# Latent attention: the value products of a head's last two tiles, with their gates, behind the next head's scores

## The chip, the cores and the metric

The kernel runs on one core of a Trainium2 chip. Times are device microseconds (us) from launch to end. TensorE (PE) does matrix products and transposes into PSUM, an accumulation memory of eight banks here; VectorE (DVE), ScalarE (ACT) and GpSimd (POOL) work on what stands in PSUM (GpSimd only on SBUF) and in SBUF. Each engine takes its own instructions in the order in which the program lists them and waits at semaphores for the others.

## The reference, cut to what matters

Two layers: first multi-head latent attention (MLA), then sparse attention. The change is in the first. For 512 tokens and 16 heads it computes, after low-rank projections and norms:

```python
def causal_block_attention(q, k, v, scale):
    for start in range(0, S, Q_BLOCK):          # four tiles of 128 queries
        s = jnp.einsum('bqhd,bkhd->bhqk', q[:, start:end], k[:, :end]) * scale
        p = jax.nn.softmax(jnp.where(mask, s, -jnp.inf), axis=-1)
        outs.append(jnp.einsum('bhqk,bkhd->bqhd', p.astype(v.dtype), v[:, :end]))
...
    o = causal_block_attention(q, k, v, MLA_QK ** -0.5)
    o = o.reshape(B, S, MLA_HEADS * MLA_V) * jax.nn.silu(z)
    return o @ w_out
```

## The kernel before

The program is a list of instructions per engine, written by hand; nothing is reordered by a scheduler. Products that need more than one pass of precision are done by `mm3` (lines 93 to 95): high by high, high by low and low by high part. So each weight and each activation is split into a high part (ScalarE, a copy) and a low part (VectorE or GpSimd, raw minus high).

The 16 heads run as a pipeline over steps h = 0 to 15. Each step works on three heads at once and on four tiles i = 0 to 3 of 128 tokens:

- `scores(h, a, i)` (L684 to L690): products of queries by keys into one of two banks. scores(h, 0) waits for the low parts of head h's four tiles (`x_free`).
- `turn(h + 1, i)` (L674): transposes of the next head's normed queries and keys.
- `values(h, i)` (L707): i + 1 products of transposed probabilities by values into a single bank, `o_bank`. It waits for the transposed probabilities (`pt_ready`) and for the gate of the tile before it (`o_free`), which reads that bank.
- `turn_probs(h, i)` (L699): i + 1 transposes of the probabilities, after their exponential.
- `project(h + 2, a, i)`: 15 products that make queries, keys and values of the head after the next; tile t waits for `p_free` of tile t - 2.

`split_weights(h + 3)` makes that head's weights in high (ScalarE L985) and low parts (VectorE L1356), in the steps 0 to 12. Heads after 15 don't exist: from step 14 nothing is projected, in step 15 nothing is turned.

On VectorE, a step does for each tile: `maximum` (L1379) of the scores, `low(h + 1)` (L1373), in tile 0 the split of the weights, in tile 1 `probs_out(h, 0)` (L1384, probabilities to SBUF), from tile 2 on `gate(h, i - 2)` (L1389 reciprocal of the row sum, L1392 product with the silu path) and `scale(h + 2, i - 1)` (L1364, L1366: norm factor and gain on queries and keys). At a step's end follow probs_out(h, 3), gate(h, 2), scale(h + 2, 3), gate(h, 3). The factor of a scale comes from GpSimd (L1221, L1222), which needs the squares that ScalarE sums over the projection (L993, L995). GpSimd also rotates the scaled queries (L1234 to L1239), two tiles at a time. On ScalarE, a tile of a step is `exponential` (L1009), `high(h + 1)` (L1002), in tile 0 the split, then probs_out of tiles 1 and 2 (L1015) and `stats(h + 2)`.

Of `step` on TensorE the end is:

```python
                        turn_probs(h, 3)
                        if h == H - 1:
                            turn_o(0)
                        values(h, 2)
                        if h == H - 1:
                            turn_o(1)
                        values(h, 3)
```

`turn_o` (L738) transposes the gated output for the output projection.

Of the kernel before, what the change touches and what calls it, by code (L numbers as in the profile page):

```python
# [32 lines left out]
H = 16  # L33
# [64 lines left out]
def trunk(nc, x, positions, inv_freq, norm_g, mla_w_in, mla_g_cq, mla_w_uq, mla_g_ckv, mla_w_ukv,  # L98
          mla_g_q, mla_g_k, mla_w_out, nsa_w_in, nsa_g_q, nsa_g_k, nsa_pe_k, nsa_w1_k, nsa_w2_k,
          nsa_pe_v, nsa_w1_v, nsa_w2_v, nsa_w_out, out):  # L100
    with ExitStack() as whole:
# [281 lines left out]
        with ExitStack() as layer:  # L383
            z_sb = at_slab("z_sb", 0, [P, NT, ZZ])
            with ExitStack() as ctx:
# [197 lines left out]
                def _(pe):  # L583
# [64 lines left out]
                    def project(n, a, t):  # L648

                        if t == 0:  # L650
                            pe.wait_ge(wh_ready, n + 1)
                        if n == 0 and t == 0:
                            pe.wait_ge(c_lo_made, KQ + KKV)
                        if 4 * n + t > 1:
                            pe.wait_ge(p_free, 4 * n + t - 1)
                        tok = slice(t * P, (t + 1) * P)
                        for k in range(KQ):
                            mm3(nc, p_bank[t % 2][:, 0:WQ], (c_hi[:, k, tok], c_lo[:, k, tok]),
                                (wq_of(wh_hi[a], k), wq_of(wh_lo[a], k)), start=k == 0, stop=k == KQ - 1)
                        for k in range(KKV):  # L660
                            last = mm3(nc, p_bank[t % 2][:, WQ:WQ + WKV],
                                       (c_hi[:, KQ + k, tok], c_lo[:, KQ + k, tok]),
                                       (wkv_of(wh_hi[a], k), wkv_of(wh_lo[a], k)), start=k == 0, stop=k == KKV - 1)
                        last.then_inc(p_done, 1)

                    def turn(n, t):

                        if t % 2 == 0:
                            pe.wait_ge(qk_rotated, 2 * n + t // 2 + 1)
                        if 4 * n + t > 1:  # L670
                            pe.wait_ge(x_free, 4 * n + t - 1)
                        for part in range(4):
                            src = (qn, kn)[part // 2][:, t, (part % 2) * HQK:(part % 2 + 1) * HQK]
                            last = nc.tensor.transpose(x_bank[t % 2][0:HQK, part * P:(part + 1) * P], src, ident[:, :])  # L674
                        last.then_inc(x_done, 1)

                    def scores(h, a, i):
                        if i == 0:
                            pe.wait_ge(x_free, 4 * h + 4)
                        if h == 0 and i == 0:  # L680
                            pe.wait_ge(z_left, NT * (NCH - 2))
                        tok, keys = slice(i * P, (i + 1) * P), (i + 1) * P

                        dst = score_bank[i % 2]  # L684
                        for part in range(2):
                            mm3(nc, dst[:, 0:keys], (qkT_hi[a][:, part, tok], qkT_lo[a][:, part, tok]),
                                (qkT_hi[a][:, 2 + part, 0:keys], qkT_lo[a][:, 2 + part, 0:keys]),
                                start=part == 0, stop=False)
                        nc.tensor.matmul(dst[:, tok], identb[:, :], causal[:, :], start=False,
                                         stop=True).then_inc(s_done, 1)  # L690

                    def turn_probs(h, i):


                        pe.wait_ge(exp_done, 4 * h + i + 1)
                        if i == NT - 1:
                            pe.wait_ge(pt_ready, 4 * h + i)
                        for j in range(i + 1):
                            last = nc.tensor.transpose(pt_bank[:, j * P:(j + 1) * P],  # L699
                                                       prob[:, i % 2, j * P:(j + 1) * P], ident[:, :])  # L700
                        last.then_inc(t_done, 1)

                    def values(h, i):
                        pe.wait_ge(pt_ready, 4 * h + i + 1)
                        pe.wait_ge(o_free, 4 * h + i + 1)
                        for j in range(i + 1):
                            last = nc.tensor.matmul(o_bank[:, 0:DV0], probT[:, i % 2, j * P:(j + 1) * P],  # L707
                                                    v_all[:, j, h * DV0:(h + 1) * DV0], start=j == 0, stop=j == i)
                        last.then_inc(pv_done, 1)

                    def step(h, a, x, p):
                        for i in range(NT):
                            scores(h, a, i)
                            if x:
                                turn(h + 1, i)
                            if i >= 2:
                                values(h, i - 2)
                            if i >= 1:
                                turn_probs(h, i - 1)
                            if p:  # L720
                                project(h + 2, a, i)
                        turn_probs(h, 3)
                        if h == H - 1:
                            turn_o(0)
                        values(h, 2)
                        if h == H - 1:
                            turn_o(1)
                        values(h, 3)

                    def turn_o(k):  # L730

                        if k == 0:
                            pe.wait_ge(p_free, 4 * H)
                        if k >= 4:
                            pe.wait_ge(o_lo_made, k - 3)
                        pe.wait_ge(o_free, 4 * k + 5)
                        for t in range(NT):
                            last = nc.tensor.transpose(bank[4 + k % 4][:, t * P:(t + 1) * P],  # L738
                                                       z_sb[:, t, k * P:(k + 1) * P], ident[:, :])
                        last.then_inc(o_turned, 1)  # L740
# [544 lines left out]
                def _(dve):  # L1285
# [68 lines left out]
                    def split_weights(n, a):  # L1354
                        dve.wait_ge(wh_hi_made, n + 1)
                        nc.vector.tensor_tensor(wh_lo[a][:, :], wh_raw[:, :], wh_hi[a][:, :].bitcast(F32),  # L1356
                                                ALU.subtract).then_inc(wh_ready, 1)
# [12 lines left out]
                    def low(n, a, t):  # L1370
                        dve.wait_ge(x_hi, 4 * n + t + 1)
                        at = slice(t * P, (t + 1) * P)
                        nc.vector.tensor_tensor(qkT_lo[a][:, :, at],  # L1373
                                                x_bank[t % 2][0:HQK, :].rearrange("p (a t) -> p a t", a=4),
                                                qkT_hi[a][:, :, at].bitcast(F32), ALU.subtract).then_inc(x_free, 1)

                    def maximum(h, a, i):
                        dve.wait_ge(s_done, 4 * h + i + 1)
                        nc.vector.tensor_reduce(negmax[:, a, i:i + 1], score_bank[i % 2][:, 0:(i + 1) * P], AX.X,  # L1379
                                                ALU.max, negate=True).then_inc(max_done, 1)  # L1380
# [6 lines left out]
                    def gate(h, a, i):  # L1387

                        o.link(nc.vector.reciprocal(rinv[:, i:i + 1], rowsum[:, a, i:i + 1]))  # L1389
                        dve.wait_ge(pv_done, 4 * h + i + 1)  # L1390
                        at = z_sb[:, i, h * DV0:(h + 1) * DV0]
                        nc.vector.scalar_tensor_tensor(at, o_bank[:, 0:DV0], rinv[:, i:i + 1], at, ALU.mult,  # L1392
                                                       ALU.mult).then_inc(o_free, 1)

                    def step(h, a, x, p):
                        for i in range(NT):
                            maximum(h, a, i)
                            if x:
                                low(h + 1, 1 - a, i)
                            if i == 0 and h + 3 < H:  # L1400
                                split_weights(h + 3, 1 - a)
                            if i == 1:
                                probs_out(h, 0)
                            if i >= 2:
                                gate(h, a, i - 2)
                            if p and i >= 1:
                                scale(h + 2, i - 1)
                        probs_out(h, 3)
                        gate(h, a, 2)
                        if p:  # L1410
                            scale(h + 2, 3)
                        gate(h, a, 3)


                    nc.vector.memset(rinv[:, :], 1.0).then_inc(o_free, 1)
# [494 lines left out]
```

## Time and profile before

| | us |
|---|---|
| median of 3 runs | 1056.43 |
| the three runs | 1054.86, 1056.43, 1056.91 |
| the profiled execution | 1056.62 |
| its span, first to last instruction | 1054.8 |
| TensorE busy in the span | 1009.9 |
| VectorE, ScalarE, GpSimd busy | 454.8, 398.8, 407.5 |

The span is 1.8 us shorter than the time of its own execution. The kernel's first 165 us are loads, the input projection and the projection of the first two heads. The heads' steps follow until about 431 us, then the output projection, the second layer's input projection, its attention and its output projection. A "start" below is in us from the span's start. Matmuls are pipelined: one of 128 rows by 128 columns is listed with about 0.27 us, but the next one starts 0.11 us after it, and the profile counts the longer figure as busy. An fp32 product of that size is recorded as two instructions, so that the eight of values(h, 3) stand for four products.

### The profile page before, as it was taken

The numbers are of one execution on the slowest core, as the hardware profiler recorded it, in microseconds if no ns is written. First come the engines' busy times: TensorE is split into PE (matmuls) and PEld (weight loads), VectorE is DVE, ScalarE is ACT, GpSimd is POOL, SyncE is SP. The second block draws the span as 40 slices with busy tenths as digits, with TensorE's granted clock in tenths as the row PEclk, the third lists the DMA queues.
The fourth block names the chain that finished last, engine by engine and source line by source line (L and its number), as shares of the span: only waits on it lengthen the run. The fifth ranks groups of instructions, "written<-read, shape, count | busy, mean of one in ns | idle before, by whom it ended". The sixth has DMA issues, their size and how long they took to land. (4 is left out here: it accounts for less than half of the span.)

```text
span 1054.8 us, 16083 instructions
## 1 busy us (share of the span) xinstructions
PE 1009.9 (96%) x6262; PEld 867.6 (82%) x6262; DVE 454.8 (43%) x1217; ACT 398.8 (38%) x948; POOL 407.5 (39%) x548
## 2 busy tenths in 40 slices
PE   4999998999999998999999999999989999999898
PEld 4988888989898987788888877788868888888776
DVE  3331025666656655321111114667645555555511
ACT  4263245555555544431342122344323333333210
POOL 1444436454555543234344234657621111111131
PEclk8999999999999999999999999999989999999899
DMA  5332131101010110222372212222200000000031
GB/s 178 108 120 80 53 93 42 44 22 44 23 43 23 44 41 2 80 80 80 106 153 77 79 40 75 86 85 80 81 1 1 1 1 1 2 1 2 1 109 52
DMA packets 42454, 58.89 MB, mean 56 GB/s; under 512 B 8821, under 2 KB 25482, under 8 KB 42378
## 3 DMA queue, kind: packets, MB, share of 16 engines
q1 hardware_dynamic: 40672, 57.42, 17.5%
q8 instruction: 50, 0.82, 0.3%
q10 hardware_dynamic: 1706, 0.43, 0.2%
q14 instruction: 26, 0.21, 0.1%
HBM read 55.62 MB, written 2.10 MB: 55 GB/s over the span
## 5 line engine op out<-in xcount | busy, mean ns | idle before, releaser
L93 PE MATMUL bank<-w_hi,h_hi 128*128 128x512 f32 (+2 forms) x480 | 188.4, 393 | 6.7 <-DVE h_lo L1295 6.7
L1253 POOL TENSOR_TENSOR w_lo<-w_raw,w_hi 128x2048 fp32r<-128x2048 f32 (+1 forms) x26 | 118.6, 4560 | 173.9 <-ACT w_hi L1039 173.9
L94 PE MATMUL bank<-w_lo,h_hi 128*128 128x512 f32 (+2 forms) x480 | 184.4, 384 | 0.0
L95 PE MATMUL bank<-w_hi,h_lo 128*128 128x512 f32 (+2 forms) x480 | 184.3, 384 | 0.0
L93 PEld LDWEIGHTS bank<-w_hi,h_hi 128*128 128x128 f32 x480 | 91.3, 190 | 26.0 <-DVE w_lo L1290 6.9
L95 PEld LDWEIGHTS bank<-w_hi,h_lo 128*128 128x128 f32 x480 | 91.2, 190 | 17.1
L94 PEld LDWEIGHTS bank<-w_lo,h_hi 128*128 128x128 f32 x480 | 91.4, 191 | 15.5
L93 PE MATMUL bank<-w_hi,c_hi 128*128 128x192 f32 (+1 forms) x320 | 93.8, 293 | 3.3 <-DVE kn L1366 3.3
L95 PE MATMUL bank<-w_hi,c_lo 128*128 128x192 f32 (+1 forms) x320 | 88.8, 278 | 0.0
L94 PE MATMUL bank<-w_lo,c_hi 128*128 128x192 f32 (+1 forms) x320 | 88.5, 276 | 0.0
L1774 POOL TENSOR_TENSOR o_c<-o_c,o_sw 128x256 f32<-128x256 f32 x16 | 11.8, 735 | 186.1 <-DVE o_c L1840 186.1
L1695 PE MATMUL bank<-kvr,probT 128*128 128x65 f32 x640 | 82.1, 276 | 0.0
L1039 ACT ACTIVATE w_hi<-w_raw 128x2048 fp32r<-128x2048 f32 (+1 forms) x26 | 49.2, 1891 | 85.7 <-PE bank L95 85.7
L93 PE MATMUL bank<-w_hi,o_hi 128*128 128x512 f32 x192 | 78.1, 407 | 2.3 <-PEq L1869 1.9
L1695 PEld LDWEIGHTS bank<-kvr,probT 128*128 128x128 f32 x640 | 76.9, 193 | 0.0
L95 PE MATMUL bank<-w_hi,o_lo 128*128 128x512 f32 x192 | 76.5, 398 | 0.0
L94 PE MATMUL bank<-w_lo,o_hi 128*128 128x512 f32 x192 | 76.3, 397 | 0.0
L1198 POOL TENSOR_TENSOR w_lo<-w_raw,w_hi 128x2048 fp32r<-128x2048 f32 (+1 forms) x11 | 46.6, 4236 | 73.9 <-ACT w_hi L926 73.9
L1373 DVE TENSOR_TENSOR qkT_lo<-bank,qkT_hi 96x512 fp32r<-96x512 f32 x64 | 43.9, 687 | 70.0 <-ACT qkT_hi L1002 70.0
L1009 ACT ACTIVATE prob<-bank,negmax 128x128 f32<-128x128 f32 (+1 forms) x64 | 33.8, 528 | 102.5 <-DVE negmax L1379 102.5
L1794 DVE TENSOR_REDUCE negmax<-bank 128x2 f32<-128x256 f32 (+2 forms) x96 | 54.7, 596 | 26.2 <-PE bank L1606 25.1
L1745 ACT ACTIVATE probT<-bank 128x512 f32<-128x512 f32 (+1 forms) x96 | 48.9, 526 | 44.6 <-PE bank L1637 43.0
(255 smaller groups left out, 2284.0 us busy)
## 6 DMA issues: line engine op xcount, KB each, us to landing
w_raw<-in_nsa_w_in SPq DMA_DIRECT2D x10, 1024.0 KB, 5.0
w_raw<-in_mla_w_in SPq DMA_DIRECT2D x8, 1024.0 KB, 5.0
w_raw<-in_mla_w_out SPq DMA_DIRECT2D x8, 1024.0 KB, 5.0
w_raw<-in_nsa_w_in SPq DMA_DIRECT2D x8, 984.0 KB, 5.0
w_raw<-in_mla_w_uq SPq DMA_DIRECT2D x16, 288.0 KB, 3.0
w_raw<-in_mla_w_ukv SPq DMA_DIRECT2D x16, 256.0 KB, 3.3
w_raw<-in_nsa_w_out SPq DMA_DIRECT2D x4, 1024.0 KB, 5.7
w_raw<-in_mla_w_in SPq DMA_DIRECT2D x4, 704.0 KB, 5.0
```

What stands on the lines that cost most here:

```text
L93: nc.tensor.matmul(out, a[0], b[0], start=start, stop=False)
L94: nc.tensor.matmul(out, a[0], b[1], start=False, stop=False)
L95: return nc.tensor.matmul(out, a[1], b[0], start=False, stop=stop)
L1009: nc.scalar.activation(prob[:, i % 2, 0:keys], score_bank[i % 2][:, 0:keys], ACT.Exp, bias=negmax[:, a, i:i + 1], accum_out=rowsum[:, a, i ...
L1039: nc.scalar.activation(w_hi[g % 2][:, :, 0:width], w_raw[g % 2][:, :, 0:width], ACT.Copy).then_inc(m_hi, 1)
L1198: nc.gpsimd.tensor_tensor(w_lo[g % 2][:, :, 0:width], w_raw[g % 2][:, :, 0:width], w_hi[g % 2][:, :, 0:width].bitcast(F32), ALU.subtract). ...
L1253: nc.gpsimd.tensor_tensor(w_lo[g % 2][:, :, 0:width], w_raw[g % 2][:, :, 0:width], w_hi[g % 2][:, :, 0:width].bitcast(F32), ALU.subtract). ...
L1373: nc.vector.tensor_tensor(qkT_lo[a][:, :, at], x_bank[t % 2][0:HQK, :].rearrange("p (a t) -> p a t", a=4), qkT_hi[a][:, :, at].bitcast(F32 ...
L1695: last = nc.tensor.matmul(o_most[:, i, b, :] if i < 3 else o_last[:, b, :], probT[n % 2][:, at:at + P], kvr[:, j, c0:c0 + DV1], start=j == ...
L1745: nc.scalar.activation(probT[n % 2][:, at:at + wide], score_bank[k % 3][:, 0:wide], ACT.Exp).then_inc(exp_done, 1)
L1774: o.link(nc.gpsimd.tensor_tensor(o_c[:, :, :], o_c[:, :, :], o_sw[:, :, 0, :], ALU.add))
L1794: nc.vector.tensor_reduce(negmax[:, n % 2, i, b0:b0 + nb], first_bank[k % 2][:, 0:nb * keys].rearrange("p (b c) -> p b c", b=nb), AX.X, AL ...
```

## The change

On TensorE the value products of tiles 2 and 3 of a head leave the head's end. They are issued in the next step, those of tile 2 behind scores(h + 1, 0) and turn(h + 2, 0), those of tile 3 behind scores(h + 1, 1) and turn(h + 2, 1). On VectorE their gates move likewise: gate(h, 2) behind the next step's tile 0 with its split of weights, gate(h, 3) behind the next step's maximum 1 and low 1. The last head keeps its old order. Nothing else is touched.

```diff
@@ TensorE, step
                             scores(h, a, i)
                             if x:
                                 turn(h + 1, i)
+                            if i < 2 and h:
+                                values(h - 1, i + 2)
                             if i >= 2:
                                 values(h, i - 2)
...
                         turn_probs(h, 3)
                         if h == H - 1:
                             turn_o(0)
-                        values(h, 2)
-                        if h == H - 1:
+                            values(h, 2)
                             turn_o(1)
-                        values(h, 3)
+                            values(h, 3)
@@ VectorE, step
                             if i == 0 and h + 3 < H:
                                 split_weights(h + 3, 1 - a)
+                            if i < 2 and h:
+                                gate(h - 1, 1 - a, i + 2)
                             if i == 1:
                                 probs_out(h, 0)
...
                         probs_out(h, 3)
-                        gate(h, a, 2)
                         if p:
                             scale(h + 2, 3)
-                        gate(h, a, 3)
+                        if h == H - 1:
+                            gate(h, a, 2)
+                            gate(h, a, 3)
```

On TensorE, from the end of head 0 into step 1 (x7 is the seven products of tiles 2 and 3; w_hi and c_hi belong to a projection, qkT to scores, ident with prob or qn to transposes), the difference reads:

```order
@@ -813,5 +813,4 @@
 L95 MATMUL bank<-w_hi,c_lo 128x256
 L699 MATMUL bank<-ident,prob 128x128 x4
-L707 MATMUL bank<-v_all,probT 128x128 x7
 L93 MATMUL bank<-qkT_hi_83 128x128
 L94 MATMUL bank<-qkT_lo_85,qkT_hi_83 128x128
@@ -823,4 +822,5 @@
 L674 MATMUL bank<-ident,qn 96x128 x2
 L674 MATMUL bank<-ident,kn 96x128 x2
+L707 MATMUL bank<-v_all,probT 128x128 x3
 L93 MATMUL bank<-w_hi,c_hi 128x192
 L94 MATMUL bank<-w_lo,c_hi 128x192
```

Four of the seven products (tile 3) stand one projection and one pair of scores further on.

On VectorE, the end of head 0 and the start of step 1, before the change:

```order
105 L1384 COPY probT<-bank 128x512
106 L1389 RECIPROCAL rinv<-rowsum 128x1
107 L1392 SCALAR_TENSOR_TENSOR z_sb<-bank,rinv,z_sb 128x128
108 L1364 SCALAR_TENSOR_TENSOR qn<-bank,ms_qk,gq 128x192
109 L1366 SCALAR_TENSOR_TENSOR kn<-bank,ms_qk,gk 128x128
110 L1389 RECIPROCAL rinv<-rowsum 128x1
111 L1392 SCALAR_TENSOR_TENSOR z_sb<-bank,rinv,z_sb 128x128
112 L1379 TENSOR_REDUCE negmax<-bank 128x1
113 L1373 TENSOR_TENSOR qkT_lo_85<-bank,qkT_hi_83 96x4x128
114 L1356 TENSOR_TENSOR w_lo<-w_raw,w_hi 128x1088
115 L1379 TENSOR_REDUCE negmax<-bank 128x1
```

and with it (its lines are numbered one higher, L1393 for L1392 and so on):

```order
105 L1385 COPY probT<-bank 128x512
106 L1365 SCALAR_TENSOR_TENSOR qn<-bank,ms_qk,gq 128x192
107 L1367 SCALAR_TENSOR_TENSOR kn<-bank,ms_qk,gk 128x128
108 L1380 TENSOR_REDUCE negmax<-bank 128x1
109 L1374 TENSOR_TENSOR qkT_lo_85<-bank,qkT_hi_83 96x4x128
110 L1357 TENSOR_TENSOR w_lo<-w_raw,w_hi 128x1088
111 L1390 RECIPROCAL rinv<-rowsum 128x1
112 L1393 SCALAR_TENSOR_TENSOR z_sb<-bank,rinv,z_sb 128x128
113 L1380 TENSOR_REDUCE negmax<-bank 128x1
```

Head 0's gate of tile 2, two instructions, now follows the split of the weights, and its gate of tile 3 comes four instructions after that.

## Rows read from the trace of the kernel before

**Rows 1.** The page, busy time, share of the span and instructions of each engine

```profile
PE 1009.9 (96%) x6262; PEld 867.6 (82%) x6262; DVE 454.8 (43%) x1217; ACT 398.8 (38%) x948; POOL 407.5 (39%) x548
```

**Rows 2.** One head: length; PE, PEld, DVE, ACT, POOL busy; clock; DMA share; GB/s

```profile
235.60:252.80 17.20, 16.47 (x137) 15.47 (x136) 10.69 (x27) 9.32 (x36) 8.73 (x24) 1.00 0.11 34
```

**Rows 3.** TensorE's waits from 165 to 431 us: releaser, total, times, longest

```profile
PE bank L707 <- DVE z_sb L1392: 11.5, 18, 0.7
```

**Rows 4.** Timeline of TensorE through a head: start, duration, line, operands, idle before

```profile
231.16 0.60 PE L699 MATMUL bank<-ident,prob 128*128 128x128 f32 x4
231.74 0.91 PE L707 MATMUL bank<-v_all,probT 128*128 128x128 f32 x6
233.38 1.13 PE L707 MATMUL bank<-v_all,probT 128*128 128x128 f32 x8 [0.73 <-DVE z_sb L1392]
234.26 0.30 PE L93 MATMUL bank<-qkT_hi 96*128 96x128 f32 x1
...
235.39 0.34 PE L93 MATMUL bank<-w_hi,c_hi 128*128 128x192 f32 x1
...
237.18 0.28 PE L93 MATMUL bank<-qkT_hi 96*128 96x256 f32 x1
...
238.41 0.27 PE L699 MATMUL bank<-ident,prob 128*128 128x128 f32 x1
...
248.36 0.60 PE L699 MATMUL bank<-ident,prob 128*128 128x128 f32 x4
```

**Rows 5.** Timeline of VectorE and GpSimd around the same head end

```profile
230.45 0.69 DVE L1373 TENSOR_TENSOR qkT_lo<-bank,qkT_hi 96x512 fp32r<-96x512 f32 x1 [1.33 <-ACT qkT_hi L1002]
231.06 0.15 DVE L1389 RECIPROCAL rinv<-rowsum 128x1 f32<-128x1 f32 x1
...
232.39 0.70 POOL L1222 TENSOR_TENSOR ms_qk<-ms_qk,minus_half 128x2 f32<-128x2 f32 x1
232.69 0.15 DVE L1389 RECIPROCAL rinv<-rowsum 128x1 f32<-128x1 f32 x1
232.88 0.35 DVE L1392 SCALAR_TENSOR_TENSOR z_sb<-bank,rinv,z_sb 128x128 f32<-128x128 f32 x1
233.19 0.42 DVE L1364 SCALAR_TENSOR_TENSOR qn<-bank,ms_qk,gq 128x192 f32<-128x192 f32 x1
...
233.79 0.15 DVE L1389 RECIPROCAL rinv<-rowsum 128x1 f32<-128x1 f32 x1
...
235.20 0.32 POOL L1239 TENSOR_TENSOR qn<-rotq 128x64 f32<-128x64 f32 x1
```

**Rows 6.** Timeline of VectorE and ScalarE in the next step's first tile

```profile
235.24 0.29 DVE L1379 TENSOR_REDUCE negmax<-bank 128x1 f32<-128x128 f32 x1 [0.28 <-PE bank L689]
235.56 0.37 ACT L1009 ACTIVATE prob<-bank,negmax 128x128 f32<-128x128 f32 x1 [3.36 <-DVE negmax L1379]
...
236.40 1.10 ACT L985 ACTIVATE w_hi<-w_raw 128x1088 fp32r<-128x1088 f32 x1
236.53 0.69 DVE L1373 TENSOR_TENSOR qkT_lo<-bank,qkT_hi 96x512 fp32r<-96x512 f32 x1 [1.00 <-ACT qkT_hi L1002]
...
237.54 1.30 DVE L1356 TENSOR_TENSOR w_lo<-w_raw,w_hi 128x1088 fp32r<-128x1088 f32 x1 [0.32 <-ACT w_hi L985]
...
238.75 0.42 DVE L1379 TENSOR_REDUCE negmax<-bank 128x1 f32<-128x256 f32 x1
```

**Rows 7.** Timeline of TensorE in the last two steps

```profile
416.79 0.63 PE L699 MATMUL bank<-ident,prob 128*128 128x128 f32 x4 [1.25 <-ACT probT L1015]
...
419.98 0.30 PE L93 MATMUL bank<-qkT_hi 96*128 96x128 f32 x1
```

**Rows 8.** Timeline where GpSimd's rotation and VectorE's split of weights overlap

```profile
155.36 1.38 DVE L1356 TENSOR_TENSOR w_lo<-w_raw,w_hi 128x1088 fp32r<-128x1088 f32 x1
...
155.54 1.37 POOL L1235 TENSOR_TENSOR rotq<-qn,tsin 128x64 f32<-128x64 f32 x1
```

**Rows 9.** Busy time by stretch, early in the second layer's attention (columns as rows 2)

```profile
764.00:781.00 17.00, 14.36 (x60) 9.77 (x58) 4.93 (x8) 5.92 (x9) 5.30 (x2) 0.70 0.00 1
```

## The prediction

> **What bounds the kernel now.** I read the busy table first: TensorE is busy 1009.9 of 1054.8 us, every other engine under 44% [rows 1]. So time is lost or won only where TensorE stands still. The change touches the attention of the first layer, the heads between about 165 and 431 us. There the table by stretches shows one head: 17.20 us, of which TensorE is busy 16.47, VectorE 10.69, ScalarE 9.32, GpSimd 8.73, at a granted clock of 1.00 [rows 2]. The five stretches of 17.20 us that I cut from 184 us on agree to the last digit, so the heads repeat exactly and one of them can be worked through for all. The waits of TensorE in this stage are led by one entry: the value products (L707) wait for the gate (L1392), 11.5 us in 18 times [rows 3]. That wait stands at the end of each head.
>
> The timeline of one head end shows it [rows 4]. I count everything from the start of the last probability transposes, turn_probs(h, 3), at 231.16. Four instructions of this kind take 0.44 us (0.11 each: the eight of values(h, 3) run from 233.38 to 234.26). Then values(h, 2) starts at 231.74, 0.14 late, and is issued in 6 x 0.11 = 0.66. values(h, 3) could start at 232.40 and starts at 233.38, 0.98 late: it needs the bank that gate(h, 2) frees, and that gate ends at 232.88 + 0.35 = 233.23 [rows 5]; 0.15 later TensorE goes on. So a head end loses 0.14 + 0.98 = 1.12 us. The profile names 0.73 of it, since it counts a matmul's modelled tail as busy. The check: the pieces of a head, 0.44 (transposes), 1.13 (scores 0 and turn, 234.26 to 235.39), 3.02 (first projection, scores 1, turn, 235.39 to 238.41), 9.95 (from turn_probs(h, 0) to the next turn_probs(h, 3), 238.41 to 248.36) and 0.66 + 0.88 (values) add up to 16.08, and 17.20 - 16.08 = 1.12.
>
> **Part one: what goes.** No arithmetic is added or removed; 15 pairs of value products and their gates move, with no DMA or other issue. In steps 0 to 13 the head end runs straight from the transposes into scores(h+1, 0). That needs low(h+1, 3), which ends at 230.45 + 0.69 = 231.14 [rows 5]; the scores come at 231.60, so 0.46 us are in hand and I put this wait at nothing (what would use up the 0.46 is a later high on ScalarE; bound: 0.1 us). A gain of 1.12 per head end, if nothing else waits.
>
> **Part two: what is late next.** The moved gate(h, 2) now stands on VectorE behind maximum 0, low 0 and the split of the next weights (L1356); the value products of tile 3, now after scores 1 on TensorE, wait for it, and everything on TensorE is queued behind them. When does that gate end? From turn_probs(h, 3) = 0:
> - scale(h+2, 3) starts at 233.19 - 231.16 = 2.03. It is not held by the gate ahead of it but by GpSimd's power, 232.39 + 0.70 = 233.09 [rows 5], so it does not come earlier when that gate leaves. VectorE is free at 233.79, that is 2.63.
> - maximum 0 then starts at once, since its scores are done by 0.44 + 0.94. Before, it waited for TensorE until 235.24. From there the rows run: exponential +0.32, ScalarE's split of the weights +0.84 (behind exponential and high, back to back), VectorE's split +1.14, the next instruction +1.21 [rows 6]. That is 2.63 + 3.51 = 6.14.
> - the gate: reciprocal to product 0.19 (232.69 to 232.88), product 0.35, to TensorE 0.15 [rows 4, 5], 0.68 together when the rounding of the hundredths is spread: 6.14 + 0.68 = 6.82.
> TensorE is ready for values(h, 3) at 0.44 + 1.13 + 0.66 + 3.02 = 5.25. It waits 1.57 us, in place of the 1.12 removed. The new head is 6.82 + 0.88 + 9.95 = 17.65 us against 17.20: **0.45 us longer**, for the 12 heads from turn_probs(0, 3) to turn_probs(12, 3), since split_weights runs in steps 0 to 12: 12 x 0.45 = +5.4 us. After the gate VectorE is behind by some two us, but catches up: maximum 1, low 1, gate(h, 3), probs_out 0 and scale end before TensorE asks for them at its third scores, so no second wait is added in these heads.
>
> **Part three: the last heads.** Step 13 has no split. The gate is then ready for TensorE at 2.63 + 0.32 + 0.97 (exponential to low, 235.56 to 236.53) + 0.61 (low to reciprocal, 230.45 to 231.06) + 0.68 = 5.21 [rows 5, 6], TensorE comes at 5.25: no wait, 1.12 won. In step 14 nothing is projected. TensorE comes to values(13, 3) at 5.25 - 1.79 (the projection, 235.39 to 237.18) + 0.1 = 3.55 and waits 1.66. For the other waits of these two steps I walked the queues: each engine's entries in program order, each with its duration and each release with its delay as in the rows. In step 14 that gives -1.12 (old head end), +1.65 (this wait) and -1.1, because values(14, 0) comes later and finds its probabilities nearly ready (a wait of 1.3 becomes 0.2): 13.1 in place of 13.63 between the transposes (248.36 + 9 x 17.20 = 403.16, to 416.79). Step 15: scores(15, 0) starts at 419.98, 3.19 after the transposes at 416.79; now 0.44 after. The 1.54 of values(14, 2) and (14, 3) comes back behind the scores, where it fills a wait for the exponential of about 0.3. 3.19 - 0.44 - 1.54 + 0.3 = 1.5; the walk gives 1.4. Steps 14 and 15 together: -1.95 [rows 7]. Behind turn_probs(15, 3) the order is unchanged, and later stages just shift.
>
> **The sum:** +5.4 - 1.1 - 1.95 = +2.35 us. On the profiled execution's own 1056.62 us that is 1059.0; the median of the runs, 1056.43, lies 0.19 lower. I take **1058.8 us**. The same walk with the old order gives 17.18 per head against the 17.20 of the trace, so I trust it to about 0.1 us a head, 12 x 0.1 = 1.2 us either way; with the tail's 0.3, +0.8 to +3.9.
>
> **A rule against this change.** The weights' split reads two operands from SBUF, and it moves closer to GpSimd's rotation. Rows: at 155.36, where the two overlap, the split took 1.38 instead of 1.29 to 1.30, and GpSimd's product 1.37 instead of 0.32 [rows 8]. In the heads the rotation ends at 235.20 + 0.32, 4.36 on my clock [rows 5]; the split now starts at 4.93 instead of 6.38. So 0.57 remains and the sum has nothing for it. The Trainium skill (SBUF — State Buffer, "Who interferes with whom") says that a VectorE instruction with two SBUF inputs and a GpSimd instruction that reads SBUF exclude each other, and the one that came second blocks; the row agrees. By that rule a rotation 0.6 later would hold the split, and with it TensorE, for what is left of one GpSimd product.
>
> **Rivals.**
> A, the gate comes in time (not slower). If the gate were free for TensorE by 5.25 instead of 6.82, all of the 1.12 would stay won: 14 x 1.12 = 15.7 and some 1.5 in the last two heads, 1039 us. For it speaks that VectorE is busy only 10.69 of 17.20 us. Against it: its busy share doesn't matter, the queue's order does, and every link is read from a row. The point from which it decides: per head even at 0.45 less, in total even at 0.20 less (2.35 / 12). Full gain 3%; between them (the chain up to 0.4 shorter, 1052 to 1056) 5%.
> B, the chain is longer than the sum, since it is now all on the path: the collision above, at most a GpSimd product of 0.32 per head, 12 x 0.32 = 3.8, giving 1062.6; or the probabilities of the next head waiting too. 10%.
> C, the clock. In the second layer TensorE had a granted clock of 0.70 from 764 to 781 us [rows 9]; half clock is 1.2 GHz, so it lost up to 0.30 x 17 = 5.1 us there. Where such a stretch begins can move with the shift of 2 us, and the runs before differ by 2.05 us (1054.86 to 1056.91). This is no result of the change but widens it by about 1.5 us.
>
> **How the numbers follow.** The likeliest is the forecast, the wait moved and 0.45 longer, 82%: 1058.8, its own range 1056.5 to 1061. A holds 8%, B 10%. The range that holds 8 in 10: 1055.8 to 1061.8. 0.2% is 2.1 us, about what can be told from no change, and my sum lies right at it. The forecast's 82% therefore splits in two: 42% within 0.2%, 40% above. B adds its 10% to slower. A gives 6% faster (below 1054.3) and 2% within. So faster 0.06, same 0.44, slower 0.50.
>
> **What would show it.** In the profile after: a head of 17.6 us instead of 17.20; L707's wait for the gate still the first entry of TensorE's waits, 13 long ones of about 1.2 us by the profile's count (some 0.4 of the 1.57 hidden by the modelled tail); that wait in front of the eight products only, none before scores 0; VectorE's maximum 0 directly behind scale 3; the split's start 4.9 us after the last transposes; step 13 about 16.1 us. Wrong would make it: heads of 16.1 us throughout (A), a split of VectorE that starts later than 5.1 or takes over 1.3 (B), or a second wait, at probs_out 0 or at a projection.

## The result and the profile after

Over 16 runs each, the changed kernel takes 1061.53 us at the median, the kernel before 1056.16. The medians lie 5.4 us apart. The ratio on record, which is not the plain quotient of the two medians, is 1.0041 with a 95% interval of 1.0027 to 1.0055, so 0.41% slower, 4.3 us; the heads of the two profiles, below, differ by 5.1 us. The profiled execution took 1062.37 us, with a span of 1060.6 us.

The waits of TensorE in the heads come first. In the rows, an engine's instruction waits for another's; then the total, the number of times and the longest:

```profile
PE bank L707 <- DVE z_sb L1393: 20.0, 14, 1.9
PE bank L93 <- DVE qkT_lo L1374: 1.3, 1, 1.3
```

The wait of [rows 3] is still there, for the same gate, and instead of 11.5 us it now takes 20.0. It has fewer and longer parts: 14 times up to 1.9 us in place of 18 times up to 0.7. The second row is one wait, of the first scores of all, at 166.50; the kernel before has it too (1.25 us at 165.43).

One head by stretch (columns as in [rows 2]), then the stretch of step 14 and four single microseconds inside it:

```profile
251.90:269.64 17.74, 16.28 (x136) 15.41 (x135) 10.72 (x28) 9.32 (x35) 8.78 (x24) 1.00 0.10 32
...
409.97:424.37 14.40, 11.14 (x76) 9.88 (x75) 8.03 (x22) 6.08 (x20) 2.94 (x9) 0.88 0.00 1
...
416.00:417.00 1.00, 1.00 (x9) 1.00 (x9) 0.18 (x1) 0.79 (x3) 0.00 (x0) 0.90 0.00 0
417.00:418.00 1.00, 1.00 (x4) 1.00 (x4) 0.96 (x4) 0.00 (x0) 0.00 (x0) 0.50 0.00 0
419.00:420.00 1.00, 1.00 (x7) 0.99 (x6) 0.28 (x1) 0.68 (x3) 0.00 (x0) 0.50 0.00 0
420.00:421.00 1.00, 1.00 (x6) 0.87 (x5) 0.50 (x1) 0.79 (x2) 0.00 (x0) 0.89 0.00 0
```

A head takes 17.74 us, not 17.20, with a clock of 1.00. In step 14 the granted clock falls to 0.50, which is 1.2 GHz, for about 3.4 us.

The timeline of one head of the kernel after, TensorE first, then the other engines (start, duration, engine, line, operands, idle before). It answers to [rows 4 to 6]:

```profile
251.91 0.60 PE L699 MATMUL bank<-ident,prob 128*128 128x128 f32 x4
...
253.48 0.83 PE L707 MATMUL bank<-v_all,probT 128*128 128x128 f32 x6
...
258.73 1.13 PE L707 MATMUL bank<-v_all,probT 128*128 128x128 f32 x8 [1.46 <-DVE z_sb L1393]
...
259.69 0.27 PE L699 MATMUL bank<-ident,prob 128*128 128x128 f32 x1
...
269.65 0.60 PE L699 MATMUL bank<-ident,prob 128*128 128x128 f32 x4
```

```profile
253.15 0.70 POOL L1223 TENSOR_TENSOR ms_qk<-ms_qk,minus_half 128x2 f32<-128x2 f32 x1
...
253.95 0.42 DVE L1365 SCALAR_TENSOR_TENSOR qn<-bank,ms_qk,gq 128x192 f32<-128x192 f32 x1 [0.42 <-POOL ms_qk L1223]
...
254.54 0.28 DVE L1380 TENSOR_REDUCE negmax<-bank 128x1 f32<-128x128 f32 x1
...
254.85 0.37 ACT L1010 ACTIVATE prob<-bank,negmax 128x128 f32<-128x128 f32 x1 [1.89 <-DVE negmax L1380]
...
255.69 1.11 ACT L986 ACTIVATE w_hi<-w_raw 128x1088 fp32r<-128x1088 f32 x1
...
256.83 1.29 DVE L1357 TENSOR_TENSOR w_lo<-w_raw,w_hi 128x1088 fp32r<-128x1088 f32 x1 [0.32 <-ACT w_hi L986]
...
258.04 0.16 DVE L1390 RECIPROCAL rinv<-rowsum 128x1 f32<-128x1 f32 x1
...
258.23 0.35 DVE L1393 SCALAR_TENSOR_TENSOR z_sb<-bank,rinv,z_sb 128x128 f32<-128x128 f32 x1
```

Read the chain upwards from 258.73. The eight products start 0.15 after the gate's end (258.23 + 0.35). The gate stands directly behind the split, the split waits for ScalarE's part, ScalarE's part stands behind exponential and high, the exponential waits for maximum 0, and maximum 0 starts at once behind the scale, which waits for GpSimd. From the transposes at 251.91 to 258.73 it is 6.82 us.

The time from the last transposes of one head to those of the next, through the stage:

| interval between the x4 transposes | before | after |
|---|---|---|
| heads 0 to 12, twelve intervals | 12 x 17.20 = 206.40 | 213.24 |
| of these: head 2 to 3 | 17.20 | 18.10 |
| of these: the nine from head 3 on | 17.20 | 17.74 or 17.75 |
| head 12 to 13 | 17.20 | 16.10 |
| head 13 to 14 | 13.63 | 14.40 |
| head 14 to 15 | 10.49 | 9.04 |
| sum, head 0 to 15 | 247.72 | 252.78 |

That is +5.06 us in the heads, of the 5.8 us between the two spans. The rest is a later arrival at head 0 by 1.07 (180.63 against 179.56), less 0.3 behind the heads. The later arrival is not the change's: a second profile of the changed kernel arrives at 179.45.

Below, step 13, 14 and 15 stand for the intervals of head 12 to 13, 13 to 14 and 14 to 15, and a scale 3 that VectorE lists at the end of a step runs at the start of the next interval: that of step 13 in head 13 to 14.

### The profile page after: what moved, and what is told of

It is laid out like the page before. It is cut to its first block and busy times, and to the rows that moved or that the text cites. A ratio compares the mean times of both kernels' runs of the same rounds, so it can differ in the third digit from the quotient of the medians.

```text
span 1060.6 us, 16083 instructions
## 1 busy us (share of the span) xinstructions
PE 1007.3 (95%) x6262; PEld 867.7 (82%) x6262; DVE 454.8 (43%) x1217; ACT 398.9 (38%) x948; POOL 408.1 (38%) x548
## 5 line engine op out<-in xcount | busy, mean ns | idle before, releaser
L707 PE MATMUL bank<-v_all,probT 128*128 128x128 f32 x320 | 47.7, 280 | 20.0 <-DVE z_sb L1393 20.0
```

## Experiments

### The gate ahead of the split

```diff
                             if x:
                                 low(h + 1, 1 - a, i)
+                            if i == 0 and h:
+                                gate(h - 1, 1 - a, 2)
                             if i == 0 and h + 3 < H:
                                 split_weights(h + 3, 1 - a)
-                            if i < 2 and h:
-                                gate(h - 1, 1 - a, i + 2)
+                            if i == 1 and h:
+                                gate(h - 1, 1 - a, 3)
```

> The changed kernel with one difference on VectorE: gate(h-1, 2) stands ahead of the weights' split of tile 0, not behind it; TensorE's order is that of the changed kernel. Theory (the gate queued behind the split is what TensorE waits for): the gate is there 5.21 us after the last transposes of the head, TensorE comes at 5.25, so no wait at the eight products, heads of 16.1 to 16.2 us in place of 17.74, and 16 us less than the kernel before: about 1040 us. Rival (the hand-over of the single bank from tile 2 to tile 3 costs TensorE its wait wherever the gate stands): heads stay at 17.2 us or more, 1056 us or more. Second rival (the split itself comes late for the next projection now): no wait at the products, but one of 0.3 us or more before a projection, heads of 16.5.

Measured: 1041.09 us at the median, ratio to before 0.9850 (0.9826 to 0.9874). The heads take 16.10 to 16.14 us (head 2 to 3: 16.47). The table by stretch for one head, and the wait for the gate over all heads:

```profile
261.56:277.66 16.10, 16.10 (x136) 15.39 (x135) 10.62 (x28) 9.32 (x35) 8.63 (x24) 1.00 0.13 37
...
PE bank L707 <- DVE z_sb L1393: 2.5, 4, 1.9
```

TensorE is busy all of the head. The gate comes only just in time: it ends at 266.26 + 0.35 = 266.61, and the eight products start at 266.76, 0.15 later, the delay that they have behind a gate elsewhere. TensorE's order is that of the changed kernel, so the handing over of the bank from tile 2 to tile 3 is free; what cost the time was the place of two VectorE instructions behind a third. Both rivals fall. Step 14 took 14.70 us, not the 13.1 that my walk gives, with a wait of 1.9 us and a clock of 0.88, both as in the changed kernel, where the step takes 14.40.

### Both gates behind the maximum

```diff
                             maximum(h, a, i)
+                            if i < 2 and h:
+                                gate(h - 1, 1 - a, i + 2)
                             if x:
                                 low(h + 1, 1 - a, i)
                             if i == 0 and h + 3 < H:
                                 split_weights(h + 3, 1 - a)
-                            if i < 2 and h:
-                                gate(h - 1, 1 - a, i + 2)
```

> As the one before, but both moved gates stand right behind the maximum of tile 0 and of tile 1, ahead of low. Theory: the gate is there about 1.8 us earlier than TensorE needs it, so the heads are the same 16.1 us, and only step 14, where TensorE comes early, gains: 12.2 to 12.6 us between its transposes in place of 13.1. In all 17 us less than before: 1039 us. If the gate in front of low delays the low parts, a wait shows at scores or at the turn of a head, and the heads are longer than in the run with the gate behind low.

Measured: 1035.77 us, ratio 0.9810 (0.9785 to 0.9834). All heads take 16.02 us, step 14 12.52, and TensorE waits for the gate 0.7 us in all:

```profile
243.30:259.32 16.02, 16.02 (x136) 15.38 (x135) 10.72 (x28) 9.32 (x35) 8.78 (x24) 1.00 0.12 36
...
PE bank L707 <- DVE z_sb L1393: 0.7, 3, 0.3
```

This is the fastest version tried, 20 us under the kernel before: same instructions as the changed kernel, with two of VectorE's in another place. It is 3 us faster than expected. Against the run before, 5.3 us at the median, the two profiles show 3.8 us in the heads (233.65 and 229.82 from head 0 to 15): 1.3 from the other heads, 0.1 shorter each, 2.2 from step 14, whose low clock is absent here, and 0.3 from the late start in head 2 (explained under the changed kernel's second profile), which is now covered. Most of the 0.1 is in the eight products: with the gate well ahead they take 0.89 (248.49 to 249.38), where with the gate just in time they take 0.96 (266.76 to 267.72). The rest of the 5.3 I can't place.

### Only tile 3 moves

```diff
+                            if i == 0 and h:
+                                values(h - 1, 3)
...
                         turn_probs(h, 3)
...
                         values(h, 2)
-                        values(h, 3)
```

On VectorE gate(h, 2) stays at the head's end and gate(h, 3) moves behind the next maximum 0; the last head keeps its old order.

> Half of the change: the value products of tile 2 and their gate stay at the head's end, as before; only those of tile 3 move, and only behind the next head's first scores, with their gate behind maximum 0. Theory (the loss at a head's end is the wait of tile 3 for tile 2's gate, which 1.1 us of scores and turn can fill): the 0.14 before the products of tile 2 stay, the 0.98 goes: heads of 16.2 to 16.3 us, 15 us less than before, about 1041.5 us. Rival (a gate at the head's end costs TensorE the wait, whatever stands between): heads of 17.2.

Measured: 1040.77 us, ratio 0.9854 (0.9831 to 0.9877), heads of 16.21 to 16.23 us, for one of them the transposes from start to start:

```profile
261.52 0.60 PE L699 MATMUL bank<-ident,prob 128*128 128x128 f32 x4
...
277.73 0.60 PE L699 MATMUL bank<-ident,prob 128*128 128x128 f32 x4
```

As expected on each point: 0.14 of the old loss stays, 0.98 goes. So 1.1 us of cover is enough for that hand-over, and the gain needs neither the second projection nor the second scores in between.

### A longer split, in both kernels

```diff
+                        if n > 3:
+                            spare = w_lo[a][:, :, :].rearrange("p k c -> p (k c)")[:, 1088:1488]
+                            nc.vector.tensor_tensor(spare, wh_raw[:, 0:400], wh_hi[a][:, 0:400].bitcast(F32),
+                                                    ALU.subtract)
                         nc.vector.tensor_tensor(wh_lo[a][:, :], wh_raw[:, :], wh_hi[a][:, :].bitcast(F32),
                                                 ALU.subtract).then_inc(wh_ready, 1)
```

> The kernel before with a longer split of the weights on VectorE: from head 4 on a second subtraction of 400 columns, whose result nobody reads, stands in front of the real one (some 0.45 us by the 1.30 for 1088 columns), in 12 steps. Theory: in this kernel nothing that TensorE needs soon stands behind the split, and about 0.5 us are in hand, so heads stay at 17.2 and the time at that of before, within 1 us. Rival (VectorE's own work per head is on TensorE's path in both kernels): 12 x 0.45 = 5 us more.

> The changed kernel with the same longer split. Theory: the split now stands between the last transposes and the gate that TensorE waits for, so every bit of it counts: heads of 17.74 + 0.45 = 18.2 us, 5 to 6 us more than the changed kernel, about 1066.5 us. Rival (the gate's wait hangs on something else of the chain): less than 2 us more.

The added instruction, as the first of these two runs shows it, with the real split behind it:

```profile
240.48 0.58 DVE L1358 TENSOR_TENSOR w_lo<-w_raw,w_hi 128x400 fp32r<-128x400 f32 x1 [0.32 <-ACT w_hi L985]
240.97 1.28 DVE L1360 TENSOR_TENSOR w_lo<-w_raw,w_hi 128x1088 fp32r<-128x1088 f32 x1
```

It holds VectorE for 0.49 us. In the kernel before, heads grew from 17.20 to 17.32 to 17.34, and the time to 1057.37 us (ratio 1.0015, 0.9997 to 1.0034): nearly all of it is hidden, though 0.13 per head is not, so the slack was below the half microsecond that I gave it.

The profile of this run took 1062.23 us, 4.9 above the median of its runs. Its heads don't explain that: two stretches at half clock do, from 167.2 to 170.6 and from 423.2 to 430.1, the second in step 15:

```profile
423.22 2.05 PE L707 MATMUL bank<-v_all,probT 128*128 128x128 f32 x8 [0.60 <-DVE z_sb L1396]
...
420.91:434.29 13.38, 11.37 (x58) 9.95 (x59) 5.15 (x17) 4.92 (x12) 4.52 (x1) 0.74 0.24 80
```

The waits just ahead of the second were 1.26, 0.17 and 0.60 us, and the one ahead of the first 1.25. In the profile of the kernel before the same waits stand at the same places, the clock stays at 1.00, and step 15 takes 10.49.

In the changed kernel, heads of undisturbed clock grew from 17.74 to 18.22, that is by 0.48, the whole of it. So far the theory holds. But the time rose to 1078.53 us (ratio 1.0196, 1.0171 to 1.0220), 17 us and not 5 to 6. The timeline and two neighbouring heads by stretch say why:

```profile
265.28 1.13 PE L707 MATMUL bank<-v_all,probT 128*128 128x128 f32 x8 [1.94 <-DVE z_sb L1397]
...
257.98:277.78 19.80, 17.86 (x137) 17.00 (x136) 11.22 (x29) 9.30 (x35) 9.26 (x24) 0.91 0.09 29
277.78:296.00 18.22, 16.28 (x136) 15.40 (x135) 11.21 (x29) 9.30 (x35) 9.25 (x24) 1.00 0.11 32
```

The first of the two heads lost 1.58 us more at a mean clock of 0.91. Of the twelve intervals eight are like it (19.76 to 19.86) and four like the second. With the wait of 1.46 us in the changed kernel not one head was, in two profiles; with 1.94 two of three are, in one. The added half microsecond was so paid about three times over.

### The changed kernel again

> The changed kernel again, for a second profile. Expected: heads of 17.74 us again, all twelve; step 13 16.1, step 15 9.0. In the first profile step 14 took 14.40 us with a granted clock of one half from 415.0 to 418.4. If that stretch belongs to this kernel, it is there again and the median of these runs is 4 to 5.5 us above before; if it comes and goes, the profile or some of the runs lack it, and step 14 is then 13.1 us. Head 2 took 18.10 because VectorE began a scale 0.36 us late; I expect that at another place or not at all.

Measured: 1061.03 us, ratio 1.0047 (1.0030 to 1.0064). The profile repeats the first within a few hundredths: heads of 17.74 and 17.75, head 2 to 3 again 18.10, step 13 16.11, step 14 14.39 with its low clock, step 15 9.04. (In the first profile that stretch is from 416.8 to 420.2, by its rows above, and not from 415.0 to 418.4 as the expectation has it.) My expectation that head 2 would not repeat was wrong. The late start is that of scale 3, here in step 13 of the first profile:

```profile
411.21 0.70 POOL L1223 TENSOR_TENSOR ms_qk<-ms_qk,minus_half 128x2 f32<-128x2 f32 x1
412.36 0.42 DVE L1365 SCALAR_TENSOR_TENSOR qn<-bank,ms_qk,gq 128x192 f32<-128x192 f32 x1 [0.78 <-POOL ms_qk L1223]
```

GpSimd ends at 411.91, and VectorE starts 0.45 later, where it takes 0.10 in the head shown above (253.85 to 253.95). It does so in steps 2 and 13 alone, in the changed kernel (twice), in both runs with other places of the gate, and in the filled one below. In the kernel before, with and without the longer split, and with tile 3 alone, where gate(h, 2) stands ahead of scale 3, no step shows it; nor does the changed kernel with the longer split.

### VectorE's stream shifted

```diff
+                    for _ in range(12):
+                        o.link(nc.vector.memset(rinv[:, :], 1.0))
                     nc.vector.memset(rinv[:, :], 1.0).then_inc(o_free, 1)
```

> The changed kernel with 12 small memsets of VectorE ahead of the heads, in idle time of that engine, which shift all of its later instructions in its stream. In three profiles with the moved gates (and the run with the gates behind the maximum) scale 3 starts 0.36 us late in step 2 and step 13 and nowhere else, and in both kernels with gate 2 ahead of scale 3 never. If that hangs on the place in VectorE's instruction stream, the two late starts are gone or in other steps; head 2 is then 17.74 and step 14 at 14.0. If it hangs on the step's own work or data, they stay in steps 2 and 13. The median moves by less than 1 us either way.

Measured: 1058.06 us, ratio to before 1.0013 (0.9998 to 1.0027). The late starts are gone, in all 14 steps it is 0.10 or 0.11; all twelve heads take 17.73 or 17.74, and step 14 falls to 13.08 us, lower than the 14.0 expected, since its low clock is gone too. The median lies 3.0 to 3.5 us under the changed kernel's two, where I had expected less than 1. The heads give 1.75 of it (251.03 against 252.78 from head 0 to 15). Another 1.7 lies behind the last transposes of the heads (625.5 us to the end against 627.2), where the order is the same and the ten profiles range from 624.1 to 627.6; that part I can't explain. The wait and the stretch of step 14:

```profile
413.50 1.13 PE L707 MATMUL bank<-v_all,probT 128*128 128x128 f32 x8 [1.57 <-DVE z_sb L1393]
...
408.30:421.38 13.08, 9.92 (x76) 8.50 (x75) 7.85 (x22) 6.04 (x20) 2.93 (x9) 1.00 0.00 0
```

So the late start hangs on the place in VectorE's stream, not on what the step does. What causes it no row shows; that stays open.

### TensorE filled in step 14

```diff
+                            if i == 1 and h == H - 2:
+                                pe.wait_ge(p_free, 4 * H)
+                                fill(6)
+                            if i == 3 and h == H - 2:
+                                fill(2)
                             if i < 2 and h:
                                 values(h - 1, i + 2)
...
+                        if h == H - 2:
+                            fill(6)
                         turn_probs(h, 3)
```

> The changed kernel with 14 products of the identity by itself, whose result nobody reads, into a free bank in step 14: 6 ahead of the value products of tile 3, 2 before the next wait, 6 before the last transposes. They take 1.3, 0.45 and 1.3 us of waits of 1.9, 0.5 and 1.3 us, so by themselves they cost nothing or a little. Theory (TensorE's standing still in step 14 brings the stretch at half clock that three of three profiles with the 1.9 us wait show there, and no profile without it): no half-clock stretch near 413 us, step 14 at 13.4 to 13.6 us in place of 14.4, the median 1 us below the changed kernel. Rival (the stretch comes from something earlier or by its own period): it is there, step 14 stays at 14.4 us or grows by what the products cost.

Measured: 1058.15 us, ratio 1.0019 (1.0006 to 1.0032), about 3 us below the changed kernel's two medians, where 1 was expected. The filling, the wait that is left, and the step by stretch:

```profile
411.77 1.50 PE L713 MATMUL bank<-ident 128*128 128x128 f32 x12
413.86 0.35 PE L707 MATMUL bank<-v_all,probT 128*128 128x128 f32 x1 [0.58 <-DVE z_sb L1404]
...
408.31:421.74 13.43, 12.85 (x105) 11.79 (x103) 7.85 (x22) 6.04 (x20) 2.93 (x9) 1.00 0.00 1
```

The late start of VectorE is still there (step 14 is 13.43, 0.35 above the 13.08 of the shifted stream), the products start at the same distance from the transposes as in the changed kernel (5.55 and 5.56), and yet the clock stays at 1.00 and the step is 0.97 us shorter. So the low clock of step 14 cost 0.97, and of these orders only those in which TensorE stands still for 1.9 us there show it. That the standing still is the whole cause isn't shown: the filled version and the shifted one were profiled once each, and the profile of the longer split in the kernel before has half clock behind waits of 1.3 us and less. Of the other 2 us of the median, the profile shows 3.1 behind the heads (624.1 us against 627.2), in its own execution of 1056.66, which is 1.5 under its median; no edit touches that part.

## Why the prediction was right, and where it was small

The direction, the mechanism and the head were right, and the time lies in the range. Point by point:

- The loss of 1.12 at a head's end and its going: right. With the gate in time, heads are 16.02 to 16.14, as the 16.08 of the sum.
- No wait at scores(h + 1, 0): right, the waits list none but that of the very first scores, which both kernels have.
- The gate ready 6.82 after the transposes: measured 6.82, each link within 0.02. The wait 1.57 by my count, 1.46 by the profile's; I had said 1.2 there, since I took too much off for the matmul's tail.
- The head of 17.65: measured 17.74. The term that was short is that of the eight products. I took 0.88 from [rows 4], where scores follow them; ahead of the transposes they take 0.96 (258.73 to 259.69), after a wait of whatever length, from the gate just in time (266.76 to 267.72) to 1.93 us (415.53 to 416.49), and 0.89 where the gate is long done. 12 x 0.09 = 1.1 us.
- Step 13 at 16.1: 16.10. Steps 14 and 15: predicted 13.1 and 9.1, measured 14.40 and 9.04. Step 14 is where the sum failed most, by 1.3 us: 0.35 is the late start of VectorE, 0.97 the clock. Without these two the step takes 13.08.
- Head 2: 0.36 by the same late start.

Together 1.1 + 1.3 + 0.36 = 2.8, against 5.06 - 2.35 = 2.7 missing in the heads. The late starts I could not have read: no step of the kernel before shows one. The clock I named as rival C, but looked for it in the second layer; it fell in the very stage that the change gives longer waits. Rival A's price was right to 4 us (1039 against 1035.8 and 1041.1 us) and is reached by moving the gate. Rival B's collision between GpSimd and the split did not come: the split kept its 1.29 us. The stated tolerance of 0.1 us a head was used up to 0.09. That the time stayed in the range is in part luck: 1061.53 lies 0.3 under its upper end, and 1.7 of the missing 2.8 us (0.35, 0.36 and 0.97) are things for which the sum had no term.

The version with the stream shifted is the nearest to what I had predicted: ratio 1.0013, some 2.2 us over the median before, 3.3 by the heads (251.03 against 247.72). So without the late starts and the low clock the change would lie within what can hardly be told from no change, as the sum said.

## What to carry to other kernels

When a product is moved behind other work to cover a wait, look where its partner on the other engine lands in that engine's queue, and add up the whole chain in front of it, from the last thing that engine really waits for; a busy share of 60% says nothing about it. Move the short instruction on which the bounding engine waits ahead of the long one on which nobody waits yet: here two places in the list were worth 26 us between 1061.5 and 1035.8. And expect a wait of TensorE that grows to cost more than its length: it can bring a lower clock for the work behind it, as the wait of 1.94 us did in eight of twelve heads and that of 1.46 in none. The length alone doesn't decide it, as the profile with half clock behind waits of 1.3 us and less shows.

## What the runs showed of the hardware

- Waits of 1.46 us once per 17.74 us head, and one of 1.82, left the clock at 1.00; waits of 1.94 us once per 18.22 us head brought a stretch of half clock, about 1.6 us of loss, in eight of twelve. In step 14, with little work between waits, one of 1.9 us brought it in all three profiles, one of 1.57 didn't, nor did one of 1.9 us that idle products filled down to 0.58. But in the one profile of the kernel before with a longer split, about 7 us of half clock followed waits of 1.26, 0.17 and 0.60 us, which the kernel before passed at 1.00. So no length of a wait is shown to be safe.
- VectorE started one instruction 0.36 us late at two fixed places of its stream, 11 heads apart, the same in five profiles (the changed kernel twice, both other places of the gate, step 14 filled), gone when 12 small instructions were put ahead, and in the run with a longer split too.
- Delays from the end on one engine to the start on the other: VectorE to TensorE 0.15, VectorE to ScalarE 0.03, GpSimd to VectorE 0.10.
- Eight products of 128 columns, from their start to that of the next: 0.96 us ahead of transposes when released by a gate, 0.89 when the gate was long done; 0.88 ahead of scores after a wait of 0.73.
